# HGRN stage of a two-layer decoder step: outer products by groups of 32 rows, read-outs between weight tiles, and matmuls on constants around three turns

## What is computed

```
def step(S, inp):
    qc, kc, vc, lf = inp
    G = jnp.cumsum(lf, axis=2)
    Gl = G[:, :, -1]
    o_inter = jnp.einsum('bhik,bhkv->bhiv', qc * jnp.exp(G), S)
    ...
    o = o_inter + jnp.einsum('bhij,bhjv->bhiv', A, vc)
    S = S * jnp.exp(Gl)[..., None] + jnp.einsum('bhjk,bhjv->bhkv', kc * jnp.exp(Gl[:, :, None, :] - G), vc)
    return S, o
```

## Time and profile before

| | |
|---|---|
| runs | 2317.75 us median (2316.18 to 2320.46) |
| the profiled execution | 2314.56 us, of which the span is 2309.3 us |
| TensorE matmul busy | 2239.2 us (97%), 20556 records |
| VectorE, ScalarE, GpSimd busy | 1498.0, 1268.5, 1091.6 us |
| mean HBM traffic | 197 GB/s |
| `hgrn_block`, first layer | 151.48 us to the start of the next block at 194.65 us |
| `hgrn_block`, second layer | 1288.61 us to 1331.43 us |

### The profile page before, as it was taken

How to read it: one execution, slowest core, us unless ns; L and a number is a source line. 1 busy time by engine, 2 the same in 40 slices (tenths; PEclk the granted TensorE clock), 3 DMA queues, 4 the chain that set the end, 5 groups by cost and what they waited for, 6 DMA issues and landing times. The chain is left out here.

```text
span 2309.3 us, 57987 instructions
## 1 busy us (share of the span) xinstructions
PE 2239.2 (97%) x20556; PEld 2070.7 (90%) x20556; DVE 1498.0 (65%) x3064; ACT 1268.5 (55%) x2439; POOL 1091.6 (47%) x990
## 2 busy tenths in 40 slices
PE   7999999999999999999999999999999999999998
PEld 4967779999998899999989586899999988999997
DVE  3876339943226878888668663599322297887885
ACT  3652225576557855555556422455765596555554
POOL 0231018864446656566304110498444474665661
PEclk8999999999999999999999999999999999999999
DMA  7472135555554289899544802455555634998993
GB/s 291 156 251 98 58 137 182 175 200 184 186 190 147 96 266 308 276 309 312 196 169 153 297 5 103 148 184 181 198 188 185 196 108 134 315 311 274 311 306 129
DMA packets 124246, 457.09 MB, mean 198 GB/s; under 512 B 13792, under 2 KB 14304, under 8 KB 122976
## 3 DMA queue, kind: packets, MB, share of 16 engines
q1 hardware_dynamic: 105696, 388.37, 48.0%
q0 software_dynamic: 18432, 67.12, 10.5%
HBM read 450.94 MB, written 4.49 MB: 197 GB/s over the span
## 5 line engine op out<-in xcount | busy, mean ns | idle before, releaser
L462 POOL TENSOR_TENSOR parts<-ring,parts 128x512 fp32r<-128x512 f32 x358 | 464.1, 1299 | 470.1 <-ACT parts L455 455.3
L455 ACT ACTIVATE parts<-ring 128x512 fp32r<-128x512 f32 x616 | 387.5, 633 | 349.9 <-PE ps_u L509 281.3
L505 PE MATMUL ps_u<-h_parts,parts 128*128 128x256 f32 x4096 | 563.8, 280 | 1.1 <-ACT parts L455 0.6
L2766 PE MATMUL ps_y<-act_parts,parts 128*128 128x256 f32 x4096 | 562.5, 279 | 0.0
L505 PEld LDWEIGHTS ps_u<-h_parts,parts 128*128 128x128 f32 x4096 | 514.7, 188 | 3.8 <-ACT parts L455 2.3
L2766 PEld LDWEIGHTS ps_y<-act_parts,parts 128*128 128x128 f32 x4096 | 514.8, 188 | 0.8 <-ACT parts L2696 0.7
L462 DVE TENSOR_TENSOR parts<-ring,parts 128x512 fp32r<-128x512 f32 x258 | 185.3, 724 | 359.9 <-ACT parts L455 337.6
L2817 POOL TENSOR_TENSOR act_parts<-big,act_parts 128x256 fp32r<-128x256 f32 x256 | 246.3, 962 | 303.0 <-ACT act_parts L2795 303.0
L509 PE MATMUL ps_u<-h_parts,parts 128*128 128x256 f32 x2048 | 323.0, 279 | 1.0 <-DVE parts L462 0.7
L2770 PE MATMUL ps_y<-act_parts,parts 128*128 128x256 f32 x2048 | 322.6, 279 | 0.0
L509 PEld LDWEIGHTS ps_u<-h_parts,parts 128*128 128x128 f32 x2048 | 275.3, 188 | 2.0 <-DVE parts L462 1.1
(11 more groups left out here) (412 smaller groups left out, 2818.5 us busy)
## 6 DMA issues: line engine op xcount, KB each, us to landing
ring<-in_stream SPq DMA_DIRECT2D x503, 512.0 KB, 4.2
more_ring<-in_stream SPq DMA_DIRECT2D x126, 512.0 KB
extra_ring<-in_stream SPq DMA_DIRECT2D x32, 512.0 KB, 6.5
mod_ring<-in_stream SPq DMA_DIRECT2D x32, 512.0 KB, 3.3
big<-in_stream SPq DMA_DIRECT2D x16, 512.0 KB, 11.6
ring<-in_lead SPq DMA_DIRECT2D x6, 512.0 KB, 3.4
out_state_out<-big SPq DMA_DIRECT2D x2, 1440.0 KB, 6.9
big<-in_state SPq DMA_DIRECT2D x2, 1280.0 KB, 8.1
```

The costliest lines, as they stand in the source:

```text
L455: eng.activation(m.parts[:, q % PARTS, 0, :], half_tile(m, t, half), ACT.Copy).then_inc(s["hi_ready"], 1)
L462: eng.tensor_tensor(m.parts[:, q % PARTS, 1, :], half_tile(m, t, half), m.parts[:, q % PARTS, 0, :].bitcast(F32), ALU.subtract).then_inc(m ...
L505: pe.matmul(out, hi[:, k, :], hr[:, side, kk, 0:tokens], start=(kk + side == 0), stop=False)
L2766: pe.matmul(ps[:, half * KD // 2 + k, :], hi[:, k, :], act_parts[:, j % AHEAD, side, :], start=False, stop=False)
```

## The change

- `products` works by groups of 32 tokens: a contraction of 32 rows, 4 masked copies (256 columns), and each of the four groups writes its own bank of `ps_outer`. Masks repeat every 32 tokens, so `mask_v` needs 4 activations for 128 tokens, and its two buffers hold all of the prompt. The samples' masked values have a buffer of their own.
- `read_samples` and `read_states` are cut into pieces of 16 logical matmuls and put between tiles and distances. The order on TensorE is written anew. The last `turn` stands behind the last read-out, and `sample_products` is cut in two.
- ScalarE makes the kept states (16 activations of 128 x 64) instead of GpSimd, and copies the prompt's last state before the last turn.
- `keep_busy` takes as many columns as its output has. It is called with 8 matmuls of 192 columns ahead of turns 1 and 2, in columns 320 to 511 of a bank of `ps_sums` that nobody reads, and with 4 of 512 columns behind turn 3.

```diff
-        pe.matmul(out, operand[:, 0:P], operand, start=True, stop=True)
+        mm = pe.matmul(out, operand[:, 0:P], operand[:, 0:out.shape[-1]], start=True, stop=True)
+    return mm
...
+            def mask_v(tt):
+
+                values = vtok[:, tt, :].rearrange("p (h v) -> p h v", h=4)
+                for j in range(GROUP):
+                    i = act.activation(vm[:, tt, :, j, :], values, ACT.Copy, scale=m.mix("block_rows")[:, j:j + 1])
+                i.then_inc(s["vm_ready"], 1)
...
             mask_v(0)
+            mask_v(1)
             copy_rows(act, m, s, ada_rows, ps_mod, 1)
             copy_columns(act, m, s, ps_mod, 1, 1)
-            mask_v(1)
-            mask_v(2)
-            mask_v(3)
+            mask_samples()
+            for pair in range(A_PAIRS):
+                for b in range(NB):
+                    t = NP + NS * b + NS - 1
+                    i = act.activation(m.states[:, pair, 1 + b, :], m.state0[:, pair, b, :], ACT.Copy,
+                                       scale=since[:, pair, t:t + 1])
+                i.then_inc(s[f"kept{pair}"], 1)
             copy_rows(act, m, s, ada_rows, ps_mod, 2)
...
-        @block.gpsimd
-        def _(pool):
-            for pair in range(A_PAIRS):
-                last = blocks(since, True, NS - 1, NS)[:, pair, :, :].broadcast_to([P, NB, HD])
-                pool.tensor_tensor(m.states[:, pair, 1:, :], m.state0[:, pair, :, :], last, ALU.mult).then_inc(
-                    s[f"kept{pair}"], 1)
...
-            def products(step):
-                pe.wait_ge(s["vm_ready"], step + 1)
+            def products(tt, first, end):
+
+                pe.wait_ge(s["vm_ready"], tt + 1)
                 for pair in range(A_PAIRS):
-                    if step >= 2:
-                        pe.wait_ge(s[f"after{pair}"], HALF * (step - 1))
-                    for r in range(2):
-                        rows = slice(r * HD, (r + 1) * HD)
-                        mm = pe.matmul(ps_outer[rows, (2 * step + pair) % 4, :], ktt[:, step // 2, pair, rows],
-                                       vm[:, step % 2, 2 * pair + r, :, :], start=True, stop=True)
-                    mm.then_inc(s["u_ready"], 1)
...
+                    if tt:
+                        pe.wait_ge(s[f"after{pair}"], GROUP * end)
                 for pair in range(A_PAIRS):
+                    for group in range(first, end):
+                        tokens = slice(32 * group, 32 * group + 32)
+                        for r in range(2):
+                            rows = slice(r * HD, (r + 1) * HD)
+                            mm = pe.matmul(ps_outer[rows, group, pair * GROUP * HD:(pair + 1) * GROUP * HD],
+                                           ktt[tokens, tt, pair, rows], vm[tokens, tt, 2 * pair + r, :, :], start=True, stop=True)
+                mm.then_inc(s["u_ready"], 1)
```

More of the change, by code:

```diff
@@ L1141, in hgrn_block @@
     HALF = TB // 2
+    GROUP = 32 // C
     with signals(nc, m, names) as s, nc.psum_tensor("ps_sums", [P, 3, 512], F32) as ps_sums, \
@@ L1147, in hgrn_block @@
         after = f.take(A_PAIRS, BLOCKS, HD)
-        vm = f.take(2, 4, TB // 2, HD)
+        vm = f.take(2, 4, GROUP, HD)
+        vms = f.take(4, NB, HD)
         pair_p = f.take(2, 2 * NP)
@@ L1187, in _, with mask_samples @@
                 act.activation(vtok[0:n, tt, :], ps_outer[0:n, tt, 2 * P:4 * P], ACT.Copy).then_inc(s["kt_out"], 1)
[L1189 to L1199, removed]
+            def mask_v(tt):
[3 more added lines that the diff above has]
+                i.then_inc(s["vm_ready"], 1)
+            def mask_samples():
+                n = NB * NS
+                values = vtok[0:n, 2, :].rearrange("p (h v) -> p h v", h=4)
+                for b in range(NB):
+                    i = act.activation(vms[0:n, :, b, :], values, ACT.Copy, scale=m.mix("batch_rows")[0:n, b:b + 1])
                 i.then_inc(s["vm_ready"], 1)
@@ L1216, in _ @@
             act.activation(m.states[:, 0:A_PAIRS, 0, :], after[:, :, BLOCKS - 1, :], ACT.Copy)
[L1218 to L1223 removed]
+            copy_rows(act, m, s, ada_rows, ps_mod, 3)
+            copy_columns(act, m, s, ps_mod, 3, 3)
         @block.tensor
@@ L1249, in inter, with read_samples @@
                 return pe.matmul(out[rows], state[rows], qt[rows, pair, t:t + n], start=True, stop=True)
-            def read_samples():
-                pe.wait_ge(s["sample_free"], 1)
-                for b in range(NB):
+            def read_samples(first, end):
+                for b in range(first, end):
                     for pair in range(A_PAIRS):
@@ L1258, in read_samples, with read_states @@
                                        m.state0[:, pair, b, :])
-                mm.then_inc(s["sample_read"], 1)
-            def read_states(turn):
+                return mm
+            def read_states(turn, half):
+                first = turn * HALF + half * GROUP + 1
                 for pair in range(A_PAIRS):
-                    pe.wait_ge(s[f"after{pair}"], HALF * (turn + 1))
-                for b in range(turn * HALF + 1, min((turn + 1) * HALF + 1, BLOCKS)):
+                    pe.wait_ge(s[f"after{pair}"], first + GROUP - 1)
+                for b in range(first, min(first + GROUP, BLOCKS)):
                     for pair in range(A_PAIRS):
@@ L1282, in sample_products @@
-            def sample_products():
-                pe.wait_ge(s["vm_ready"], 5)
-                for pair in range(A_PAIRS):
[L1285 to L1290, removed]
+                    if tt:
+                        pe.wait_ge(s[f"after{pair}"], GROUP * end)
@@ new lines, in products, with sample_products @@
+                mm.then_inc(s["u_ready"], 1)
+            def sample_products(pair):
+                pe.wait_ge(s["vm_ready"], 3)
+                for other in range(A_PAIRS):
+                    pe.wait_ge(s[f"after{other}"], TB + GROUP * (pair + 1))
+                for r in range(2):
+                    rows = slice(r * HD, (r + 1) * HD)
+                    mm = pe.matmul(ps_outer[rows, pair, :], ktt[0:NB * NS, 2, pair, rows],
+                                   vms[0:NB * NS, 2 * pair + r, :, :], start=True, stop=True)
+                mm.then_inc(s["samples_u"], 1)
@@ L1302, in _ @@
             distance(2)
+            pe.wait_ge(s["sample_free"], 1)
+            read_samples(0, NB // 2)
+            distance(3)
+            read_samples(NB // 2, NB)
+            distance(4)
             ada(11, 12)
-            distance(3)
+            distance(5)
+            products(0, 0, 4)
+            distance(6)
             ada(12, 14)
-            distance(4)
+            distance(7)
             ada(14, 16)
-            distance(5)
-            products(0)
-            distance(6)
+            keep_busy(pe, m, ps_sums[:, 2, 320:512], 8)
             turn(1)
-            distance(7)
-            read_samples()
             ada(16, 20)
-            products(1)
-            ada(20, 24)
-            products(2)
-            turn(2)
[L1319 to L1327, removed]
+            pe.wait_ge(s["values_done"], 1)
+            read_states(0, 0)
+            products(1, 0, 2)
+            ada(20, 21)
+            read_states(0, 1)
+            ada(21, 23)
+            products(1, 2, 4)
+            ada(23, 24)
+            read_states(1, 0)
+            keep_busy(pe, m, ps_sums[:, 2, 320:512], 8).then_inc(s["sample_read"], 1)
+            turn(2)
+            ada(24, 26)
+            read_states(1, 1)
+            ada(26, 28)
+            sample_products(0)
+            ada(28, 29)
+            read_states(2, 0)
+            ada(29, 31)
+            read_states(2, 1)
+            ada(31, 32)
+            sample_products(1)
+            read_states(3, 0)
+            read_states(3, 1).then_inc(s["inter_ready"], 1)
             turn(3)
-            mm = read_states(3)
-            mm.then_inc(s["inter_ready"], 1)
+            keep_busy(pe, m, ps_outer[:, 3, :], 4)
         @block.vector
@@ L1372, in _ @@
             ve.sem_inc(s["values_done"], 1)
-            for turn in range(4):
-                ve.wait_ge(s["u_ready"], 2 * turn + 2)
-                for b in range(turn * HALF, (turn + 1) * HALF):
+            for first, ready in ((0, 1), (TB, 2), (TB + HALF, 3)):
+                ve.wait_ge(s["u_ready"], ready)
+                for b in range(first, TB if ready == 1 else first + HALF):
                     for pair in range(A_PAIRS):
-                        new, j = after[:, pair, b, :], b % HALF
-                        add = ps_outer[:, (2 * turn + pair) % 4, j * HD:(j + 1) * HD]
+                        new = after[:, pair, b, :]
+                        add = ps_outer[:, b // GROUP % 4, (pair * GROUP + b % GROUP) * HD:(pair * GROUP + b % GROUP + 1) * HD]
                         if b == 0:
@@ L3036, in host_layout @@
     const("eye_s", js == i_s)
-    const("block_rows", j // 8 == np.arange(P // 8)[None, :])
+    const("block_rows", j // 8 % 4 == np.arange(P // 8)[None, :] % 4)
```

4 lines of the change are left out of this document (1 added, 3 removed).

## The result

The changed kernel took 2335.73 us (2331.73 to 2343.34, 4 runs) beside 2317.31 for the kernel before (2316.18 to 2320.46): a ratio of 1.008 with a 95% interval of 1.0066 to 1.0095. Beside the last experiments it took 2337.71 us against 2317.78, again 1.008 (1.0064 to 1.0097). The forecast was 2307.9 us in a range of 2303 to 2314: wrong in its sign, by 28 us. One execution of the kernel before, beside experiments 5 to 8, took 5643.61 us and is left out of their ratios.

The account below looks back on a forecast made before the run. TensorE's list of work was taken to bound the HGRN stage from the first distance on. The terms gave -3.3 us a layer, -4.9 with the clock, -9.8 for two layers: 2317.75 to 2307.9 us, range 2303 to 2314.

Parts of the forecast that it names:

- item 8: TensorE's clock behind the last read-out: half the possible gain taken, -1.6 us a layer (bounds 0 and -3.3).
- rival A: The clock is held wherever the constants stand, in both layers: 2304.6 us; chance 0.22.
- Item 2: Outer products by row groups on TensorE: 7.5 us become 2.2 and 0.4, -4.9 us a layer.
- Item 1: GpSimd's kept states go to ScalarE, first distance moves from 154.11 to 152.9: -1.2 us a layer.
- Rival D: In the outer products, row groups wait for one another (slower): 2321.8 us; chance 0.06.
- Items 3 to 5: TensorE, per layer: cutting into pieces +0.9 us, constants ahead of turns 1 and 2 +1.0, waits for ScalarE's copies +0.8.
- Item 6: Last turn behind last read-out: leaves the last addition's path, but TensorE ends later; +0.1 us a layer.
- Item 7: Loads of tiles in the stage arrive in time at 415 GB/s: 0, up to +1.9 us.
- rival B: Tile loads become the bound, with waits ahead of tiles 22, 28 and 30: 2311.7 us; chance 0.18.
- The sum of items 1 to 7: HGRN stage of one layer without the clock's item: -3.3 us.
- Rival C: The clock gives nothing and falls at the seam as before or a little later: 2311.2 us; chance 0.17.

Follow-up runs that it names:

- experiment 5: Changed kernel plus 64 matmuls on constants a layer, at eight places, contracting over 32 rows: 2364.75 us, ratio 1.0186 to the kernel before.
- experiment 6: Changed kernel without its twenty matmuls on constants: 2330.3 us, ratio 1.0054 to the kernel before.
- experiment 7: Changed kernel plus 4 constants of 128 rows at each of eight places a layer: 2317.0 us, ratio 1.001 to the kernel before.
- experiment 8: Kernel before with kept states on ScalarE and 5 constants of 128 rows and 512 columns behind the last read-outs: 2314.04 us, ratio 0.9987.
- experiment 2: Kernel before with only the outer products by groups of 32 rows and smaller masks, at the old places: 2325.68 us, ratio 1.0026.
- experiment 4: Kernel before with only the kept states moved from GpSimd to ScalarE: 2316.87 us, ratio 0.9986.
- experiment 11: Changed kernel run again without an edit: 2337.71 us, ratio 1.008 to the kernel before.
- experiment 9: Experiment 8 with row groups for the outer products of the first 128 tokens alone: 2316.11 us, ratio 0.9992 to the kernel before.
- experiment 10: Experiment 9 plus 12 constants of 256 columns ahead of the last two groups of read-outs: 2314.57 us, ratio 0.9989 to the kernel before.
- experiment 1: Changed kernel plus 64 constants a layer of 128 rows and 256 columns, at eight places: 2323.49 us, ratio 1.0015 to the kernel before.

## Why the prediction was wrong

The step that failed is item 8, the clock, and with it the choice of cases. It looked for the clock only behind the last read-out and gave it bounds of 0 and -3.3 us. A bound on the side of a loss was missing, and no reason stood for leaving it out. The stretch at 1.2 GHz grew from 6.8 us to 37.5 in each layer. Some 33 us of it lie in the stage and took up to twice their time, so about 16 us a layer were lost where -1.6 stood. I wrote for rival A that "dense matmuls now stand in every piece of the stage"; the change in fact took dense matmuls out of it. Item 2 counted the 4.9 us of outer products as time saved and never asked what else they did. Experiments 3 and 2 show what: with the dense products put back into the changed kernel the clock holds (2319.15 us), and taking them alone out of the kernel before makes it 6 us slower. A smaller slip lies in item 8's comparison of the two levels, which set 0.92 us from start to start beside a duration of 0.61; from start to start the second group takes 0.54 (203.10 to 203.64).

- Item 1, GpSimd's kept states: right. First distance 1.34 us behind the start for 1.42; experiment 4 gives 2.7 us for 2.4, in an interval from 1 to 6.
- Item 2, row groups: right for the first 128 tokens, 1.05 us for 32 records where 1.1 was said, 33 ns a record. The two later pieces have only 16 records each, on two of the four row groups, and took just as long, 1.06 us at full clock (1326.01 to 1327.07), 66 ns a record, near the 64 of the row on two groups in the earlier trace rows. So the outer products cost 3.1 us at full clock and not 2.6, and the item was 0.5 us a layer too good: half the records on half the groups save nothing. Rival D, that row groups wait for one another, is refuted for the piece on four groups. The page "TensorE: Matmul & The Clock Gate" of the Trainium skill, Part 3, from whose 6.32 times the prediction estimated 34 ns, agrees with the trace for that piece.
- Items 3 to 5: right. Four tiles still take 1.86 us (169.36 to 171.22), the waits behind the turns are 0.32 and 0.33 us for 0.4.
- Item 6: the sign was right, the constants behind the last turn run past VectorE, but at half speed (1.49 us for the three that the trace shows).
- Item 7, the loads: part of rival B came. A tile waited 0.77 us for its load in the first layer (tile 20), where the item stood at 0; in experiment 11 the waits were 0.68 in the first layer and 1.27 and 0.75 in the second, in experiment 2 1.35. A wait is not needed for the fall: of the nine stretches of over 30 us at 1.2 GHz in the profiles, seven began in such a wait of 0.58 to 1.35 us or within 2 us behind it, and two without one (the changed kernel's second layer, experiment 5's first). It is not enough either: experiments 9 and 10 waited 0.70 to 1.20 us for loads with no fall of over 3.4 us in the 10 us behind. That it makes a fall likelier is not excluded.
- The sum of items 1 to 7: supported. The stage without the clock's loss comes out at some 39 us for 39.9 (39.3 by experiments 1 and 7), the miss of item 2 being made up by small gains in the others. Of the 38.5 us between forecast and measurement in the profiled runs (2304.8 and 2343.34), 34 lie in the two stages (55.1 and 58.3 us where 39.9 and 39.5 were forecast) and the rest in the blocks around them.
- Rival C said that the clock gives nothing, and the slower rival was D with the wrong mechanism. The one that decided, a fall amid the tiles, was not among them.

What stays open: why the row groups with the new order bring the long stretch in both layers and without it in one, in the single profile that there is, and what brought the clock back in that profile's second layer. No run separated read-outs between tiles from the moved turn. And the claim on rows rests on one pair of runs.

## What to carry to other kernels

Before taking useless but dense work off TensorE, list what is left in that stretch: if it is thin matmuls and short tiles, the engine may drop to half speed and lose more than was saved. Bound the clock's item on the side of a loss: at half speed TensorE's work takes twice as long, so the bound is the full-speed time of the work that stands behind a possible fall, here some 16 us a layer. Then run the edit with extra full-height constants beside it: when more work makes it faster, the clock is the cause. Of the constants tried here, 64 a layer with 128 rows at eight places in the thin stretch held the clock, 32 mostly did, 64 with 32 rows didn't, and the changed kernel's own twenty at three places shortened nothing. Places and numbers weren't varied apart.

## What the runs showed of the hardware that was not expected

- 64 matmuls of 32 rows and 256 columns a layer left the clock at 0.50 for 51.2 us; the same 64 with 128 rows held it at 1.00 up to the last read-outs (experiments 5 and 1, 2364.75 and 2323.49 us).
- The clock was seen to fall in the block ahead as well, just as TensorE ended 12 matmul records with 12 rows and 288 columns that took 3 us. The changed kernel's tiles at 147.88 took 0.85 us each; the same code in the profile of before kept 0.43. So this fall comes in some executions and not in others. A stretch of 3.4 to 10.2 us costs at most half of that, so it can make a part of the spread of 2310 to 2325 us; how much isn't shown.
- On two of the four row groups 16 records of outer products took 1.02 to 1.06 us at full clock, as long as 32 on all four (1.05).
- Once low, the clock stayed low from 175 to 205 us in the changed kernel, while TensorE was 97 to 100% busy.
- VectorE's 128x512 product took 695 ns without GpSimd beside it (changed kernel; 693 in experiment 4) and 1591 with it; the 128x64 one 220 and 1064.
